# Two transformer blocks on one core: who squares the differential outputs, where gates and root stand among late weight groups, and when the other stream is normed

## The chip, the cores and the metric

The kernel runs on one core of one Trainium2 chip. The metric is the device time of one launch in microseconds (us), as the median of three runs. The program is written by hand: each engine (TensorE or PE, VectorE or DVE, ScalarE or ACT, GpSimd or POOL, and the queue SP that starts weight transfers) has its own list of instructions and they meet at semaphores.

## What is computed

Two blocks follow each other on 256 tokens of width 1024, all in fp32. The change touches the first block alone. Its reference, cut to what matters:

```python
for l in range(DEPTH):                       # 2 layers; ctx first, then x; the second ctx is cut short
    co_ret  = from_heads(rms_norm(c_ret)) * silu(c_rg)
    co_diff = from_heads(rms_norm(c_diff) * (1.0 - lam_init)) * silu(c_dg)
    co_mlp  = u * (w_s @ layer_norm(v) + b_s) * silu(gate)
    # the same three branches on x: o_ret, o_diff, o_mlp
    y   = sigmoid(g_ret)*(o_ret @ w_bo[0]) + sigmoid(g_mlp)*(o_mlp @ w_bo[1]) + sigmoid(g_diff)*(o_diff @ w_bo[2])
    out = y @ w_o
    x   = x + gate * rms_norm(out, g_post[l])
```

`rms_norm` divides each head's 128 numbers by the root of their mean square.

## The kernel before

**Passes.** `PASSES` (L338) runs the first block as four passes n = 0 to 3: ctx and x of layer 0, ctx of layer 1 (only keys, values and states, "not full"), x of layer 1. So three passes are full, and only these hold the code of the change.

**Weights.** Each weight is taken in slabs of 256 x 512 (512 KB). SP loads a slab into `raw` (four slots), ACT copies it to `whi` in fp32r (`split`, L475), POOL subtracts to get the rest `wlo` (L463), and PE multiplies with the high and low parts of weights and activations: three matmuls of 512 columns for each of 2 x 2 blocks, 12 in a slab (`product`, L1455; `slab`, L1461). Four slabs make a chunk of 512 outputs, whose two PSUM banks (one for each 128 tokens) ACT copies out. ACT may split the next slab into a slot once PE has finished the slab there (`weights_used`).

**Late slabs.** In a full pass 44 slabs (11 chunks) are "late": they are dealt one by one among the attention steps, so that PE has work while ACT and DVE do softmax. The order is written out by hand, the same in all engines. `late_slab(n)` on ACT (L501) waits for PE to finish slab n and splits the slab that follows in that slot; when n is the last of a chunk (n = 3 mod 4) it first copies the chunk's two banks out, which PE needs free (`late_evacuated`, waited for in `slab`) before the next chunk's slab 0. All late chunks use the banks G[2:4]. Chunks 0 to 4 are MV, RG, DG, MU, MG; chunks 5 to 10 are the merge gates 0 to 5. Slabs 0 to 9 go beside retention, 10 to 33 beside the eight differential steps (L762), and 34 to 43 after them.

**After the differential steps (before the change).** ACT (L794 to L823) goes through slab 34, SiLU of MG, slab 35 with the copy of chunk 8, SiLU of RG, slab 36, SiLU of DG, slab 37, the square root for the head norms (`rms`, L800), slab 38, Sigmoid of gate 0, slab 39 with the copy of chunk 9 and so on. DVE (L1278 to L1301) waits for the last differential output, squares and sums it (`squares(2, 8)`, L1238 and L1239), forms the MLP branch (L1286, L1290), waits for the root, scales both normed branches by its reciprocal (L1297) and multiplies with their gates (L1301). Three increments of `branches_ready` let PE (L1772) turn the branches: 16 transposes, slab 42, 8 transposes, slab 43. ACT and DVE split the turned tiles to `ohi`, `olo` (L548, L1039).

**Merge** (L553, L1054, L1562). Six units u of two slabs: branch times `w_branch_out`, DVE multiplies with gate and adds; then `w_out`. Between the branches' split and unit 0, ACT (L819) and DVE (L1057) norm the other stream, cx or x, in passes 0 and 1, for the next pass: two squares, root, reciprocal, two products into `normed`. PE turns `normed` at the start of the next pass (L1624). `junk` and `normed` lie over the branches' buffer `o`.

Of the kernel before, what the change touches and what calls it, by code (L numbers as in the profile page):

```python
# [139 lines left out]
def build(nc, g, out):  # L140
# [14 lines left out]
    with ExitStack() as ctx:  # L155
# [311 lines left out]
        def _(act):  # L467
# [85 lines left out]
            def merge(more, in_first, final=False):  # L553
                for u in range(6):
                    act.wait_ge(weights_used, w(weights_used))
                    split(2 * (u % 2))
                    act.wait_ge(branch_out, w(branch_out, TT))
                    split(2 * (u % 2) + 1)
                    if u == 4:
                        split_high(two_kt(hhi)[0:2])  # L560
                for s in range(SLOTS):
# [63 lines left out]
            for n, (is_x, l, full) in enumerate(PASSES):  # L625
# [136 lines left out]
                for i in range(m + 2):  # L762
                    if i >= 2:
                        h, t = divmod(i - 2, TT)
                        act.wait_ge(diff_out, w(diff_out))
                        act.activation(o[:, 2, t, h * P:(h + 1) * P], G[i % 2][:, 0:P], ACT.Copy).then_inc(diff_read, 1)
                    if i < m:
# [25 lines left out]

                act.wait_ge(late_evacuated, w(late_evacuated, len(LATE) * TT))  # L794
                for i, c in enumerate((MG, RG, DG)):
                    late_slab(late + i, late_dst, G[2:4])
                    silu(c)
                late_slab(late + 3, late_dst, G[2:4])
                act.wait_ge(ss_ready, w(ss_ready))
                act.activation(rms[:], ss[:], ACT.Sqrt, bias=eps[:], scale=1.0 / P).then_inc(rms_ready, 1)  # L800
                act.wait_ge(late_evacuated, w(late_evacuated, 4 * TT))
                late_slab(late + 4, late_dst, G[2:4])
                sigmoid(0)
                late_slab(late + 5, late_dst, G[2:4], func=ACT.Sigmoid)
                sigmoid(2)
                late_slab(late + 6, late_dst, G[2:4])
                sigmoid(1)
                late_slab(late + 7, late_dst, G[2:4])
                sigmoid(3)
# [5 lines left out]
                w(late_evacuated, 2 * TT)  # L815
                if n == 0:
                    act.wait_ge(x_in, w(x_in, 16))
                if n < 2:
                    norm(cx if is_x else x)  # L819
                act.wait_ge(branches_ready, w(branches_ready, 3))  # L820
                merge(True, True, n == 3)
# [124 lines left out]
        def _(dve):  # L946
# [107 lines left out]
            def merge(gate, part, then_norm=None, direct=()):  # L1054
                split_low([ap for b in range(3) for ap in two_kt(ohi[:, b], 4)],
                          [ap for b in range(3) for ap in two_kt(olo[:, b], 4)])
                if then_norm is not None:  # L1057
                    norm(then_norm)
# [16 lines left out]
                split_low(two_kt(hhi)[2:4], two_kt(hlo)[2:4], 2)  # L1075

# [53 lines left out]
            for n, (is_x, l, full) in enumerate(PASSES):  # L1130
# [123 lines left out]
                for i in range(m + 1):  # L1254
# [14 lines left out]
                    if i == 3:  # L1269
                        link(squares(0, 0))  # L1270
# [7 lines left out]
                dve.wait_ge(diff_read, w(diff_read, m))  # L1278
                squares(2, 8).then_inc(ss_ready, 1)
                dve.wait_ge(mlp_vn, w(mlp_vn))  # L1280
# [8 lines left out]
                dve.wait_ge(gates_ready, w(gates_ready))  # L1289
                dve.tensor_tensor(o[:, 1], o[:, 1], z[:, :, MG:MG + W], ALU.mult).then_inc(branches_ready, 1)  # L1290

                dve.wait_ge(rms_ready, w(rms_ready))
                link(dve.reciprocal(rstd[:], rms[:]))
                link(dve.tensor_scalar(rstd[:, 8:16], rstd[:, 8:16], 1.0 - (0.8 - 0.6 * math.exp(-0.3 * l)), None, ALU.mult))
                for b, at in ((0, 0), (2, 8)):
                    ob = o[:, b].rearrange("p t (h n) -> p (t h) n", h=H1)
                    ins = dve.tensor_tensor(ob, ob, rstd[:, at:at + 8].unsqueeze(2).to_broadcast([P, 8, P]), ALU.mult)  # L1297
                link(ins)
                for b, gate in ((0, RG), (2, DG)):
                    dve.wait_ge(gates_ready, w(gates_ready))  # L1300
                    dve.tensor_tensor(o[:, b], o[:, b], z[:, :, gate:gate + W], ALU.mult).then_inc(branches_ready, 1)  # L1301
                w(late_evacuated, (1 + 4) * TT)
                if n == 0:
                    dve.wait_ge(x_in, w(x_in, 16))
                merge(lambda c, t: z[:, t, GATE_HOMES[c]:GATE_HOMES[c] + W], lambda t, h: z[:, t, Y_HOMES[h]:Y_HOMES[h] + W],
                      (x, cx, None, None)[n], (2, 5))
# [145 lines left out]
        def _(pe):  # L1452
# [156 lines left out]
            for n, (is_x, l, full) in enumerate(PASSES):  # L1609
# [119 lines left out]
                for i in range(m + 1):  # L1729
# [13 lines left out]
                    if i >= 1:  # L1743
# [10 lines left out]
                        if j >= 2:  # L1754
                            pe.wait_ge(diff_read, w(diff_read))
# [15 lines left out]
                pe.wait_ge(diff_read, w(diff_read, 2))  # L1771
# [196 lines left out]
```

## Time and profile before

| | |
|---|---|
| Median of three runs | 2044.94 us (2044.02 to 2046.29) |
| Profiled execution: its own time | 2043.11 us |
| Profiled execution: span of the instructions | 2041.3 us |
| Mean granted TensorE clock | 0.981 |
| PE busy | 1934.3 us (95%) |
| POOL / ACT / DVE busy | 1375.0 (67%) / 1101.8 (54%) / 614.3 us (30%) |

All times within the kernel are us from the start of the span of this one execution. A matmul's row shows about 0.39 us though the next one starts 0.23 us later, since they are pipelined; so what one slab takes is read from start to start. The three full passes come to the changed code at about 257, 569 and 936 us.

### The profile page before, as it was taken

Reading aid. Unit: us, or ns where it says so; the run is one execution under the profiler, and the core shown is the slowest. Engines: PE = TensorE matmul, PEld = TensorE weight load, DVE = VectorE, ACT = ScalarE, POOL = GpSimd, SP = SyncE. Lnnn points to the kernel's source line nnn. Section 1 sums busy time; section 2 is a strip of 40 time slices with the busy share of each in tenths; the row PEclk is TensorE's granted clock in tenths of the full one; section 3 lists DMA queues with packets and bytes.
Section 4 is the critical chain, followed back from the end, with each engine's and each line's share of the span. In section 5 each row is a group of like instructions: output and inputs, shape, how many; then the busy total and the mean of one; then the engine's idle time right before and its main releaser. Section 6 shows DMA issues by size and latency. Waiting matters only on the chain.

```text
span 2041.3 us, 26146 instructions
## 1 busy us (share of the span) xinstructions
PE 1934.3 (95%) x9524; PEld 1560.7 (76%) x9524; DVE 614.3 (30%) x1123; ACT 1101.8 (54%) x1584; POOL 1375.0 (67%) x573
## 2 busy tenths in 40 slices
PE   6999999999999799999989899999999999999997
PEld 3667877787778678777878677788888777788885
DVE  3212453512342552334325321421113331232111
ACT  3544675334574654466454874554445585555443
POOL 3656778756668667667868444678888744478884
PEclk8999999999999899999989999999999999999999
DMA  9855546744545545444546333356655633345563
GB/s 360 285 195 145 165 147 190 241 124 134 144 145 178 178 125 165 144 135 147 174 124 200 115 93 99 128 175 186 185 176 151 184 94 94 102 156 177 184 185 112
DMA packets 170816, 328.66 MB, mean 161 GB/s; under 512 B 12384, under 2 KB 13536, under 8 KB 170464
## 3 DMA queue, kind: packets, MB, share of 16 engines
q1 hardware_dynamic: 167968, 320.49, 51.3%
q10 hardware_dynamic: 2752, 6.84, 0.9%
q8 instruction: 67, 1.10, 0.2%
q14 instruction: 29, 0.24, 0.0%
HBM read 326.24 MB, written 1.05 MB: 160 GB/s over the span
## 4 chain that ended last, share of the span: by engine, by line
PE 68%; issue 12%; POOL 12%; ACT 4%; DVE 2%; DMA 2%; POOLq 0%; SPq 0%; DVEq 0%; ACTq 0%
PE G L1457 17%; PE G L1459 16%; PE G L1458 16%; POOL wlo L463 12%; PE A L1457 3%; PE A L1458 3%; PE A L1459 3%; PE A L1511 1%; ACT whi L477 1%; PE A L1548 1%; DMA raw<-in_w_in 1%; DMA modz<-in_w_mod 1%; PE A L1737 1%; ACT t L543 1%; PE G L1758 1%
## 5 line engine op out<-in xcount | busy, mean ns | idle before, releaser
L463 POOL TENSOR_TENSOR wlo<-raw,whi 128x1024 fp32r<-128x1024 f32 x568 | 1371.2, 2421 | 643.7 <-ACT whi L477 640.3
L477 ACT ACTIVATE whi<-raw 128x1024 fp32r<-128x1024 f32 x568 | 599.6, 1058 | 685.0 <-PE G L1459 567.8
L1457 PE MATMUL G<-whi,hhi 128*128 128x512 f32 (+1 forms) x1648 | 665.2, 404 | 28.9 <-DVE hlo L971 11.6
L1459 PE MATMUL G<-whi,hlo 128*128 128x512 f32 (+1 forms) x1648 | 645.9, 392 | 0.0
L1458 PE MATMUL G<-wlo,hhi 128*128 128x512 f32 (+1 forms) x1648 | 645.2, 391 | 0.0
L1457 PEld LDWEIGHTS G<-whi,hhi 128*128 128x128 f32 x1648 | 313.8, 190 | 114.9 <-issue 42.9
L1459 PEld LDWEIGHTS G<-whi,hlo 128*128 128x128 f32 x1648 | 313.6, 190 | 67.0
L1458 PEld LDWEIGHTS G<-wlo,hhi 128*128 128x128 f32 x1648 | 314.5, 191 | 59.2
L1457 PE MATMUL G<-whi,ohi 128*128 128x512 f32 x240 | 94.1, 392 | 1.0 <-issue 1.0
L1459 PE MATMUL G<-whi,olo 128*128 128x512 f32 x240 | 93.4, 389 | 0.0
L1458 PE MATMUL G<-wlo,ohi 128*128 128x512 f32 x240 | 93.4, 389 | 0.0
L1258 DVE TENSOR_REDUCE nmx<-A 128x1 f32<-128x512 f32 (+1 forms) x48 | 26.7, 597 | 137.6 <-PE A L1737 137.6
L1457 PEld LDWEIGHTS G<-whi,ohi 128*128 128x128 f32 x240 | 45.1, 188 | 10.9 <-issue 1.8
L1457 PE MATMUL A<-whi,uhi 128*128 128x512 f32 x128 | 50.0, 390 | 3.2 <-DVE ulo L1424 3.2
L1459 PEld LDWEIGHTS G<-whi,olo 128*128 128x128 f32 x240 | 45.0, 188 | 9.4
L1458 PEld LDWEIGHTS G<-wlo,ohi 128*128 128x128 f32 x240 | 45.1, 188 | 9.0
L1457 PE MATMUL A<-whi,hhi 128*128 128x512 f32 x128 | 50.5, 394 | 0.0
L1459 PE MATMUL A<-whi,hlo 128*128 128x512 f32 x128 | 49.9, 390 | 0.0
L1458 PE MATMUL A<-wlo,hhi 128*128 128x512 f32 x128 | 49.8, 389 | 0.0
L1458 PE MATMUL A<-wlo,uhi 128*128 128x512 f32 x128 | 49.8, 389 | 0.0
L1459 PE MATMUL G<-whi,ulo 128*128 128x512 f32 x128 | 49.8, 389 | 0.0
L1459 PE MATMUL A<-whi,ulo 128*128 128x512 f32 x128 | 49.8, 389 | 0.0
(369 smaller groups left out, 2255.4 us busy)
## 6 DMA issues: line engine op xcount, KB each, us to landing
raw<-in_w_in SPq DMA_DIRECT2D x332, 512.0 KB, 3.7
raw<-in_w_up SPq DMA_DIRECT2D x64, 512.0 KB, 3.7
raw<-in_w_down SPq DMA_DIRECT2D x64, 512.0 KB, 3.5
raw<-in_w_out SPq DMA_DIRECT2D x40, 512.0 KB, 3.9
raw<-in_w_branch_out SPq DMA_DIRECT2D x36, 512.0 KB, 3.9
modw<-in_w_mod SPq DMA_DIRECT2D x32, 512.0 KB, 4.9
raw<-in_w_branch SPq DMA_DIRECT2D x24, 512.0 KB, 3.5
modz<-in_w_mod SPq DMA_DIRECT2D x16, 512.0 KB, 11.0
```

Source lines behind the costliest of these rows:

```text
L463: pool.tensor_tensor(wlo[:, s], raw[:, s], whi[:, s].bitcast(F32), ALU.subtract).then_inc(lo_ready, 1)
L477: act.activation(whi[:, slot], raw[:, slot], ACT.Copy).then_inc(hi_ready, 1)
L543: act.activation(dst, A[n % 4][:, 0:dst.shape[-1]], ACT.Copy, scale=scale).then_inc(turned_copied, 1)
L1258: ins = dve.reduce_max(nmx[:, i % 2, b:b + 1], A[2 * (i % 2) + b][:, 0:nk], AX.X, negate=True)
L1457: pe.matmul(bank, hi, whi[:, slot, kk, 0:n], start=first, stop=False)
L1458: pe.matmul(bank, hi, wlo[:, slot, kk, 0:n], start=False, stop=False)
L1459: return pe.matmul(bank, lo, whi[:, slot, kk, 0:n], start=False, stop=last)
L1511: ins = pe.transpose(A[n % 4][:, b * S + t * P:b * S + (t + 1) * P], srcs[2 * (n - bank) + b](t), ident)
L1548: ins = pe.matmul(bank[at:at + 32, 0:MODN], cond[:, q * SLAB_K + kk], ring[:, i % size, kk, h * MODN:(h + 1) * MODN], start=q == 0, stop=q ...
L1737: ins = pe.matmul(bank[:, c * S:(c + 1) * S], dqT[half_p, h, t * P:(t + 1) * P], kT[half_p, h], start=True, stop=True)
L1758: ins = pe.matmul(G[j % 2][:, 0:P], aT[:, j % 2, b * P:(b + 1) * P], val[:, h * P:(h + 1) * P], start=b == 0, stop=b == nb - 1)
```

## The change

In the differential steps ACT squares each output tile from PSUM itself, with the row sum as accumulator output, right behind the copy; DVE's `squares(2, 8)` goes. After the steps ACT takes the root first, then goes through the late slabs with no table function ahead of a chunk's copies; chunk 9 (gate 4) is copied raw and gets its Sigmoid later with gates 0 and 2; the Sigmoids of gates 1 and 3 and the norm of the other stream move into the merge's units 0, 1 and 2. DVE scales the normed branches before the MLP branch, takes MG's gate last, and norms the other stream at the end of its merge. PE's waits on `diff_read` count two per output.

```diff
@@ ACT, merge
-            def merge(more, in_first, final=False):
+            def merge(more, in_first, final=False, beside=None):
                 for u in range(6):
...
+                    if beside is not None:
+                        beside(u)
@@ ACT, differential steps
                         act.activation(o[:, 2, t, h * P:(h + 1) * P], G[i % 2][:, 0:P], ACT.Copy).then_inc(diff_read, 1)
+                        act.activation(rtmp[:, 2 + t, h * P:(h + 1) * P], G[i % 2][:, 0:P], ACT.Square,
+                                       accum_out=ss[:, 8 + t * H1 + h:9 + t * H1 + h]).then_inc(diff_read, 1)
@@ ACT, after them
+                act.wait_ge(ss_ready, w(ss_ready))
+                act.wait_ge(diff_read, w(diff_read, 2 * m))
+                act.activation(rms[:], ss[:], ACT.Sqrt, bias=eps[:], scale=1.0 / P).then_inc(rms_ready, 1)
                 act.wait_ge(late_evacuated, w(late_evacuated, len(LATE) * TT))
-                for i, c in enumerate((MG, RG, DG)):
+                late_slab(late, late_dst, G[2:4])
+                for i, c in enumerate((RG, DG, MG)):
+                    late_slab(late + 1 + i, late_dst, G[2:4])
+                    silu(c)
+                for i in (4, 5):
                     late_slab(late + i, late_dst, G[2:4])
-                    silu(c)
-                late_slab(late + 3, late_dst, G[2:4])
-                act.wait_ge(ss_ready, w(ss_ready))
-                act.activation(rms[:], ss[:], ACT.Sqrt, bias=eps[:], scale=1.0 / P).then_inc(rms_ready, 1)
-                act.wait_ge(late_evacuated, w(late_evacuated, 4 * TT))
-                late_slab(late + 4, late_dst, G[2:4])
+                act.wait_ge(late_evacuated, w(late_evacuated, 5 * TT))
                 sigmoid(0)
-                late_slab(late + 5, late_dst, G[2:4], func=ACT.Sigmoid)
+                late_slab(late + 6, late_dst, G[2:4])
                 sigmoid(2)
-                late_slab(late + 6, late_dst, G[2:4])
-                sigmoid(1)
+                sigmoid(4)
                 late_slab(late + 7, late_dst, G[2:4])
-                sigmoid(3)
...
-                if n == 0:
-                    act.wait_ge(x_in, w(x_in, 16))
-                if n < 2:
-                    norm(cx if is_x else x)
+                def beside_merge(u):
+                    if u < 2:
+                        sigmoid(1 + 2 * u)
+                    if u == 2 and n == 0:
+                        act.wait_ge(x_in, w(x_in, 16))
+                    if u == 2 and n < 2:
+                        norm(cx if is_x else x)
...
-                merge(True, True, n == 3)
+                merge(True, True, n == 3, beside_merge)
@@ DVE, merge
-                if then_norm is not None:
-                    norm(then_norm)
                 for u in range(6):
...
                 split_low(two_kt(hhi)[2:4], two_kt(hlo)[2:4], 2)
+                if then_norm is not None:
+                    norm(then_norm)
@@ DVE, after the differential steps
-                        link(squares(0, 0))
+                        squares(0, 0).then_inc(ss_ready, 1)
...
-                dve.wait_ge(diff_read, w(diff_read, m))
-                squares(2, 8).then_inc(ss_ready, 1)
+                dve.wait_ge(diff_read, w(diff_read, 2 * m))
+                # here now: wait for rms_ready, reciprocal, factor, the two products o * rstd (L1292 to L1298)
...
-                dve.tensor_tensor(o[:, 1], o[:, 1], z[:, :, MG:MG + W], ALU.mult).then_inc(branches_ready, 1)
...
-                for b, gate in ((0, RG), (2, DG)):
+                for b, gate in ((0, RG), (2, DG), (1, MG)):
...
-                      (x, cx, None, None)[n], (2, 5))
+                      (x, cx, None, None)[n], (5,))
@@ PE
-                            pe.wait_ge(diff_read, w(diff_read))
+                            pe.wait_ge(diff_read, w(diff_read, 2))
...
-                pe.wait_ge(diff_read, w(diff_read, 2))
+                pe.wait_ge(diff_read, w(diff_read, 4))
```

The line that begins with # in the diff stands for four lines moved up unchanged.

## Rows read from the trace of the kernel before

**Rows 1.** Page: chain of work that ended last, share of the span.

```profile
PE 68%; issue 12%; POOL 12%; ACT 4%; DVE 2%; DMA 2%; POOLq 0%; SPq 0%; DVEq 0%; ACTq 0%
```

**Rows 2.** One stretch: busy us (x instructions), PE clock, DMA share, GB/s.

```profile
257.00:300.00 43.00, 39.81 (x195) 32.70 (x194) 23.52 (x27) 33.85 (x43) 29.95 (x12) 1.00 0.48 149
```

**Rows 3.** Waits of PE, 255 to 345: total us, times, longest.

```profile
PE G L1457 <- ACT z L509: 2.9, 2, 1.4
PE A L1511 <- DVE o L1301: 0.3, 1, 0.3
```

**Rows 4.** Timeline of PE, pass 0: start, us, instruction [idle before].

```profile
237.56 0.39 PE L1457 MATMUL G<-whi,hhi 128*128 128x512 f32 x1
...
263.88 0.39 PE L1459 MATMUL G<-whi,hlo 128*128 128x512 f32 x1
265.70 0.47 PE L1457 MATMUL G<-whi,hhi 128*128 128x512 f32 x1 [1.43 <-ACT z L509]
...
268.55 0.39 PE L1457 MATMUL G<-whi,hhi 128*128 128x512 f32 x1
...
271.26 0.39 PE L1457 MATMUL G<-whi,hhi 128*128 128x512 f32 x1
...
284.35 1.94 PE L1511 MATMUL A<-const,o 128*128 128x128 f32 x16 [0.33 <-DVE o L1301]
...
295.20 0.39 PE L1457 MATMUL G<-whi,ohi 128*128 128x512 f32 x1
...
351.32 1.09 PE L1525 MATMUL A<-const,normed 128*128 128x128 f32 x8 [0.69 <-ACT oproj L591]
```

**Rows 5.** Timeline of ACT, pass 0.

```profile
237.76 0.60 ACT L509 ACTIVATE z<-G 128x512 f32<-128x512 f32 x1 [0.63 <-PE G L1459]
...
261.64 1.06 ACT L477 ACTIVATE whi<-raw 128x1024 fp32r<-128x1024 f32 x1 [3.79 <-issue]
262.72 1.28 ACT L788 ACT_TABLE_LOAD   x1
264.01 1.06 ACT L788 ACTIVATE z<-z 128x1024 f32<-128x1024 f32 x1
264.98 1.07 ACT L509 ACTIVATE z<-G 128x512 f32<-128x512 f32 x2
...
273.84 0.31 ACT L800 ACTIVATE rms<-ss,eps 128x16 f32<-128x16 f32 x1
...
297.96 1.99 ACT L477 ACTIVATE whi<-raw 128x1024 fp32r<-128x1024 f32 x2
```

**Rows 6.** Timeline of DVE, pass 0.

```profile
257.88 3.35 DVE L1238 TENSOR_TENSOR rtmp<-o 128x1024 f32<-128x1024 f32 x1 [9.08 <-ACT o L766]
...
275.06 4.53 DVE L1297 TENSOR_TENSOR o<-o,rstd 128x1024 f32<-128x1024 f32 x2
279.62 4.58 DVE L1301 TENSOR_TENSOR o<-o,z 128x1024 f32<-128x1024 f32 x2
...
334.51 1.29 DVE L1039 TENSOR_TENSOR hlo<-A,hhi 128x512 fp32r<-128x512 f32 x2 [6.83 <-ACT hhi L548]
```

**Rows 7.** Groups of ACT's copy and square accumulator: ns min/median/max.

```profile
L766 ACT ACTIVATE o<-G x24: 256/260/268, 195.8 to 935.8; 128x128 f32<-128x128 f32 x24
...
L523 ACT ACTIVATION_READ_ACCUMULATOR junk<-x x14: 184/187/250, 295.1 to 2033.2; 128x1 f32 x14
```

**Rows 8.** Waits of ACT's exponentials, pass 0, then pass 1.

```profile
ACT e L770 <- DVE nmx L1258: 2.8, 5, 0.7
...
ACT e L770 <- DVE nmx L1258: 8.7, 5, 2.1
```

**Rows 9.** Timeline of ACT at the start: an Exp, then a Square.

```profile
10.53 0.20 ACT L621 ACTIVATE lam<-lam 128x4 f32<-128x4 f32 x1 [0.57 <-DVE lam L1089]
12.97 1.06 ACT L523 ACTIVATE junk<-cx 128x1024 f32<-128x1024 f32 x1 [2.23 <-DMA cx<-in_ctx]
```

**Rows 10.** Timeline of POOL in pass 0's merge.

```profile
299.08 24.35 POOL L463 TENSOR_TENSOR wlo<-raw,whi 128x1024 fp32r<-128x1024 f32 x10 [2.37 <-ACT whi L477]
```

More of the change, by code:

```diff
@@ L814, in _ @@
                 late_slab(late + 9, late_dst, G[2:4], func=ACT.Sigmoid)
-                w(late_evacuated, 2 * TT)
-                if n == 0:
-                    act.wait_ge(x_in, w(x_in, 16))
-                if n < 2:
-                    norm(cx if is_x else x)
+                w(late_evacuated, TT)
+                def beside_merge(u):
[5 more added lines that the diff above has]
+                        norm(cx if is_x else x)
                 act.wait_ge(branches_ready, w(branches_ready, 3))
-                merge(True, True, n == 3)
+                merge(True, True, n == 3, beside_merge)
                 if n < 3:
@@ L1277, in _ @@
                         ins.then_inc(mlp_vn, 1)
-                dve.wait_ge(diff_read, w(diff_read, m))
-                squares(2, 8).then_inc(ss_ready, 1)
-                dve.wait_ge(mlp_vn, w(mlp_vn))
+                dve.wait_ge(diff_read, w(diff_read, 2 * m))
+                dve.wait_ge(rms_ready, w(rms_ready))
+                link(dve.reciprocal(rstd[:], rms[:]))
+                link(dve.tensor_scalar(rstd[:, 8:16], rstd[:, 8:16], 1.0 - (0.8 - 0.6 * math.exp(-0.3 * l)), None, ALU.mult))
+                for b, at in ((0, 0), (2, 8)):
+                    ob = o[:, b].rearrange("p t (h n) -> p (t h) n", h=H1)
+                    dve.tensor_tensor(ob, ob, rstd[:, at:at + 8].unsqueeze(2).to_broadcast([P, 8, P]), ALU.mult).then_inc(dve_step, 1)
+                dve.wait_ge(dve_step, w(dve_step, 2))
                 dve.wait_ge(late_evacuated, w(late_evacuated, 3 * TT))
@@ L1288, in _ @@
                     link(ins)
-                dve.wait_ge(gates_ready, w(gates_ready))
-                dve.tensor_tensor(o[:, 1], o[:, 1], z[:, :, MG:MG + W], ALU.mult).then_inc(branches_ready, 1)
[L1292 to L1298, printed above, removed]
-                for b, gate in ((0, RG), (2, DG)):
+                for b, gate in ((0, RG), (2, DG), (1, MG)):
                     dve.wait_ge(gates_ready, w(gates_ready))
                     dve.tensor_tensor(o[:, b], o[:, b], z[:, :, gate:gate + W], ALU.mult).then_inc(branches_ready, 1)
-                w(late_evacuated, (1 + 4) * TT)
+                w(late_evacuated, (1 + 5) * TT)
                 if n == 0:
```

## Prediction

> **What bounds the kernel.** I read the chain of work first: two thirds of the span are PE, the rest small pieces [rows 1]. So an edit on ACT or DVE is worth only the PE pauses it ends. Next the stretch that the change touches: in 43 us from 257, PE is busy for 39.81, ACT for 33.85, DVE for 23.52, POOL for 29.95, at a granted clock of 1.00 [rows 2]; the same 43 us in the other two full passes show 39.82 both times. The stage is PE's, and 3.2 us of it are pauses. The list of PE's waits names them: twice a matmul waited for the copy of a late chunk (L509), once the transposes waited for DVE's last gate product (L1301) [rows 3]. The other two full passes have these lines with the same numbers; there is no other PE wait up to 345.
>
> **What a pause costs.** The rows overlap, so I go from start to start [rows 4]. From 268.55 to 271.26 a slab takes 2.71, 0.226 a matmul. Across the first pause the starts are 263.88 and 265.70, 1.82 apart: 1.82 - 0.23 = 1.59 lost. The slab behind it takes 268.55 - 265.70 = 2.85, another 0.13: matmuls restart slowly. Together 1.72, and twice 3.44. The transposes show 0.33 idle; with the overlap of 0.39 - 0.23 = 0.16, 0.49 are lost. They start slowly anyway. A pass pays 3.44 + 0.49 = 3.93, three passes 11.8 us. That is all that the edits can win on PE here.
>
> **Why the first pause goes.** PE pauses because ACT holds the copy of chunk 8 [rows 5]: split of slab 34 at 261.64, table load 1.28, SiLU of MG 1.06, and only at 264.98 the two copies, although the first bank was done half a slab earlier. A copy that nothing precedes is early enough: at 237.76 ACT took the second bank's copy as soon as PE had finished it (idle 0.63 until then), and PE, already in the next chunk since 237.56, shows no pause [rows 4, 5]. In the new order slab 34 is followed by slab 35 with its copies. ACT idles 3.79 before 261.64, and the root now stands there: the load 1.28 and 0.31. So PE goes on at 264.11, and the second copy starts at 264.3.
>
> **The second pause** comes from the first Sigmoid in front of chunk 9's copies, a table load and 1.06 again. It goes if ACT has caught up by then. I roll ACT forward from 264.3 with 0.95 from one large activation to the next (264.01 to 264.98, [rows 5]) and slabs of 2.72. Slab 36 now runs from 264.11, 37 from 266.83, 38 from 269.55, 39 from 272.27, 40 from 274.99, 41 from 277.71 to 280.43. ACT: copy 264.3, split 264.8, load 265.8, SiLU RG 267.1, split 268.1 (due 267.0), SiLU DG 269.0, split 270.0 (due 269.8), SiLU MG 270.9, split 272.5 on time, copies 273.8 and 275.2 on time. Both pauses are gone.
>
> **The third pause.** DVE made branches ready from the root at 273.84, by two products (4.53) and two gate products (4.58) [rows 5, 6]. Now the root ends near 259.8; DVE no longer spends 3.35 and the reduction after it on squares, and has its products done by 265.3, the MLP branch by 267.6. Then it follows ACT's gates: RG 268.1, DG 270.0, MG 271.9, each with one product of at most 3.4 (the slow one of each pair), so the last is ready by about 275.5. PE asks at 280.43. Margin 5 us.
>
> **What is late next.** After slab 39: split 275.7, load 276.7, Sigmoid 0 at 278.0, split 279.0 (due 277.9), Sigmoids 2 and 4, split 281.8 (due 280.6). Splits 1.2 us late do no harm: a slot has three slabs of 2.72 = 8.2 us between its release and its use, of which split and POOL take 1.06 + 2.43 (24.35 over 10, [rows 10]), 4.7 us of slack. ACT then starts the four high parts at 282.8, 2.3 behind the transposes' start, against 1.6 now. PE's second transposes need DVE's first low part at 284.9, after slab 42; it ends at 282.8 + 0.6 + 0.7 = 284.1. That margin, 0.8 us, is the thinnest of the plan. I cost it at nothing; if ACT is 1.5 us later than I think, it costs 0.7 a pass.
>
> **The squares on ACT.** Each adds a 128x128 activation of 0.26 and an accumulator read of 0.19, 0.45 us [rows 7], 24 times: 10.8 us of ACT. That is the upper bound if all of it were exposed; zero is the lower. Behind the copy ACT waits for DVE's maxima anyhow: in pass 0 five waits, 2.8 in total, up to 0.7; in pass 1 five, 8.7 in total, up to 2.1 [rows 8]; pass 3 has 2.1 for the longest too. These hold 0.45 each except at one or two steps of pass 0, where 0.3 to 0.45 shift splits with slack. Who waits behind it on ACT is the exponential, then DVE's mix, then transposes two slabs later. PE's doubled count on `diff_read` refers to outputs two steps back, some 10 us earlier. I take zero. Table loads: no Square of the trace has one in front. The first follows an Exp at 10.53 with no load between [rows 9], which is the case of these steps.
>
> **The merge.** Now ACT's norm (two squares, load, root, 4 us) precedes unit 0, and the split at 297.96 comes 2.5 late, for PE ended unit 0's first slab at 295.20 + 0.23 [rows 4, 5]. POOL then runs ten subtractions without a break [rows 10], and still PE waits for nothing. In unit 2 the norm delays a split by just as much, once; units 0 and 1 have 5.44 us of PE for 2.1 of splits and 0.95 of a Sigmoid. Gate 1 is needed in unit 3, gate 3 in unit 4. So the move neither wins nor loses. DVE's norm now runs behind its last split product at 334.51 + 1.29 [rows 6]; `normed` is then ready by 338 to 340, and PE turns it at 351.32 [rows 4], 11 us later. In pass 3 there is no norm. Weights' transfers follow POOL, and no queue gets more of them.
>
> **A rule of the skill that speaks against it.** A table load shows 1.28 us and the SiLU starts at 264.01, 0.01 behind its end; nothing drains in between [rows 5]. The Trainium skill, "ScalarE: Activation LUTs", section "What ACT_TABLE_LOAD costs", gives 1.28 us for the load and about 1.38 us of drain, 2.66 us a switch. By it, SiLU's and Sigmoid's loads would put the high parts 2.8 us later, and 0.7 or more a pass would be lost at PE's second transposes; the row speaks against it, and the sum goes by the row.
>
> **Sum.** -11.8 us + 0 for the squares + 0 for the merge. On the profiled execution, 2043.11 (span 2041.3 and 1.8 around it), that gives 2031.3. The median of the three runs is 1.8 above it, and their spread is 2.3; I predict on the median's scale: 2044.94 - 11.8 = 2033.1.
>
> **Rivals.**
> A (forecast, 0.72): all three pauses go: 2033.1, own range 2031 to 2036.
> B (0.16): part of it comes back. Either a copy of chunk 9 is still late, since ACT carries a backlog through three SiLUs (1.72 a pass, 5.2), or the high parts come late behind three Sigmoids (0.7 to 1.5 a pass, 2 to 4.5). For it: ACT is busy for 33.85 of 43 us, and the 0.8 us margin. Against it: splits released by PE find ACT again by slab 38. 2035 to 2038.5.
> C (0.04): a table switch costs ACT more than its row, by up to another 1.28 at each of the two loads. The high parts come 2.6 later, 1.8 past the margin: 1.8 x 3 = 5.4 of 11.8 are lost, 2038.5. Against it: the 0.01 above. This is what the skill's drain would do.
> D (0.05): nothing is won, since PE's pauses were POOL's time to catch up. POOL needs 2.43 of each 2.72 [rows 10]; if DVE's five large products, now closer together, slowed it by 1 us each, it would fall behind by more than the 4.7 of slack, and PE would stop for it. Against it: POOL is busy for 29.95 of 43 us here [rows 2] and waited 2.37 for ACT before its run of ten. 2044 to 2045.
> E (0.03), the other side: Square is not in the table set of Exp, so each of the 24 brings two loads, 2.56 more, 3.0 with its own 0.45. The exponential then starts 3.0 - 0.7 = 2.3 later in pass 0 and 3.0 - 2.1 = 0.9 later in passes 1 and 3; if PE waits each time, 8 x 2.3 + 16 x 0.9 = 33, less 11.8: 2066. It decides once more than a third of that reaches PE. Against it: rows 9.
>
> **Numbers.** The mean granted clock is 0.981 over the whole and 1.00 here [rows 2], so it is lower in places elsewhere, and how much of PE's work falls into these may change when everything after 264 comes 4 to 12 us earlier; with the runs' spread I put 2 us on either side for it. Low end: A with that, 2030.8. High end: B and C, 2038.6; outside are D, E and the tails. A measurement of this kernel tells about 0.2%, 4 us: faster (below 2040.9) holds A, B and C, 0.92; within, D, 0.05; slower, E, 0.03.
>
> **What would show it.** Right: in the stretch from 257 PE's waits on L509 and on DVE's gate product are gone, its transposes start near 280.4, the merge's first matmul comes 3.9 us earlier in pass 0, 7.9 in pass 1, 11.8 in pass 3, and all later stages keep their lengths. ACT's load of the Sqrt table lies before slab 34's split, with no load in front of a Square. Wrong: any PE wait on `ohi`/`olo` products or on POOL behind slab 41 (B, D), a load at each Square (E), a gap behind the loads (C), or a PE wait for `normed` at the pass's end.

## Result and profile after

The changed kernel takes 2032.99 us (median of 6 runs, 2027.88 to 2036.08), the kernel before, beside it on the same chip, 2044.48 (6 runs, 2039.66 to 2046.29): a ratio of 0.9948, 95% interval 0.9937 to 0.9960. The forecast was 2033.1, from a gain of 11.8 us; the medians stand 11.5 apart. The profiled execution took 2032.57, its span 2030.8.

First PE's waits in the stretch of the change. From 255 to 345 the list of the kernel after is empty; the three waits of [rows 3] are gone. The same stretch as [rows 2] (columns: stretch, length, busy us of PE, PE's weight loads, DVE, ACT, POOL, then PE clock, DMA share, GB/s):

```profile
257.00:300.00 43.00, 43.00 (x214) 36.28 (x213) 17.51 (x23) 32.02 (x45) 35.06 (x15) 1.00 0.53 162
```

PE is busy for all 43.00, where it was for 39.81; the counterpart in pass 1, from 569, reads 43.00 too. DVE has 6 us less to do; POOL has 15 instructions in the stretch, where it had 12, and 5 us more.

The page's chain of work that ended last, against [rows 1]:

```profile
PE 43%; issue 26%; POOL 26%; ACT 3%; POOLq 1%; DVE 1%; DMA 0%; DVEq 0%; ACTq 0%
```

PE's share fell from 68 to 43% and POOL's rose from 12 to 26%, in a kernel whose PE is busy for 95% as before and whose PE waits only became fewer. The chain follows whichever releaser came last, and its shares do not follow the time: of the kernels below, one that is slower than the kernel before (order alone) has the same 43 and 26%, one 9 us faster than it (the first with a held split) has 90% for PE. Nothing is read from these shares here; PE's waits decide.

ACT in pass 0, against [rows 5] (start, us, instruction, idle before):

```profile
260.61 0.26 ACT L768 ACTIVATE o<-G 128x128 f32<-128x128 f32 x1
260.77 0.27 ACT L769 ACTIVATE rtmp<-G 128x128 f32<-128x128 f32 x1
...
261.20 1.28 ACT L800 ACT_TABLE_LOAD   x1
262.50 0.31 ACT L800 ACTIVATE rms<-ss,eps 128x16 f32<-128x16 f32 x1
...
265.97 0.60 ACT L509 ACTIVATE z<-G 128x512 f32<-128x512 f32 x1 [0.25 <-PE G L1464]
267.33 0.60 ACT L509 ACTIVATE z<-G 128x512 f32<-128x512 f32 x1 [0.76 <-PE G L1464]
...
270.19 1.06 ACT L792 ACTIVATE z<-z 128x1024 f32<-128x1024 f32 x1
...
276.85 0.60 ACT L509 ACTIVATE z<-G 128x512 f32<-128x512 f32 x1 [0.30 <-PE G L1464]
278.21 0.60 ACT L509 ACTIVATE z<-G 128x512 f32<-128x512 f32 x1 [0.76 <-PE G L1464]
...
285.83 2.04 ACT L548 ACTIVATE ohi<-A 128x512 fp32r<-128x512 f32 x4
```

The root lies before all that slab 34 and those behind it put on ACT. Both pairs of copies (265.97 and 267.33; 276.85 and 278.21) now follow PE: each starts when PE has finished its bank, with ACT idle ahead of it. No table load stands in front of the Square at 260.77.

DVE, against [rows 6] (same columns):

```profile
263.40 2.36 DVE L1294 TENSOR_TENSOR o<-o,rstd 128x1024 f32<-128x1024 f32 x2
265.80 2.29 DVE L1301 SCALAR_TENSOR_TENSOR o<-A,small,z 128x128 f32<-128x128 f32 x8
271.36 1.23 DVE L1306 TENSOR_TENSOR o<-o,z 128x1024 f32<-128x1024 f32 x1 [3.28 <-ACT z L792]
273.18 6.09 DVE L1306 TENSOR_TENSOR o<-o,z 128x1024 f32<-128x1024 f32 x2 [0.59 <-ACT z L792]
286.51 2.48 DVE L1049 TENSOR_TENSOR olo<-A,ohi 128x512 fp32r<-128x512 f32 x4 [7.23 <-ACT ohi L548]
```

POOL, in the same stretch:

```profile
272.28 16.40 POOL L463 TENSOR_TENSOR wlo<-raw,whi 128x1024 fp32r<-128x1024 f32 x6 [0.92 <-ACT whi L477]
```

Six subtractions took 16.40, 2.0 more than six times the 2.40 of one that no product of DVE meets. What DVE and POOL do to each other is taken up at the end.

And PE's two groups of transposes, against [rows 4]:

```profile
283.46 1.91 PE L1516 MATMUL A<-const,o 128*128 128x128 f32 x16
...
287.95 1.03 PE L1516 MATMUL A<-const,o 128*128 128x128 f32 x8
```

**Stages of both profiled executions**, from PE's starts (us). Three marks a pass: "mix", the first matmul of the mixing (`z,wsT`); "turn", the first transpose of the branches; "end", the first transpose of the next pass (of `x` behind pass 3). "Pass 2 and its ends" runs from the first transpose of pass 2 to that of pass 3. In the kernel before the marks are at 256.87, 284.35 and 351.32 in pass 0.

```
                      before   after   difference
start to mix, pass 0  256.87  259.89   +3.02
mix to turn, pass 0    27.48   23.57   -3.91
turn to end, pass 0    66.97   66.94   -0.03
end to mix, pass 1    217.64  220.41   +2.77
mix to turn, pass 1    27.48   23.57   -3.91
turn to end, pass 1    66.97   66.95   -0.02
pass 2 and its ends    68.63   65.90   -2.73
to mix, pass 3        203.52  203.52    0.00
mix to turn, pass 3    27.48   23.57   -3.91
turn to end, pass 3    74.26   74.35   +0.09
the rest             1004.00 1002.14   -1.86
span                 2041.3  2030.8   -10.5
```

The whole gain is the three times -3.91; the other rows sum up to +1.2. Those that move by 2 or 3 are not the change's: a second profiled execution of the same changed kernel (below) has 256.64, 217.24 and 66.64 in the first, fourth and seventh. What moved them is PE's granted clock. Before the mixing of pass 0 it reads 0.50, the lower level of 1.2 GHz, from 37.15 to 47.39 in the kernel before and from 33.69 to 50.75 in the changed kernel: 6.8 us more at half speed, for the +3.02. The +2.77 and the -2.73 go the same way: 3.4 us at 0.50 before against 10.2 after, and 13.7 against 6.8.

### The profile page after: what moved, and what is told of

Its sections match the earlier page's. It is cut to its first block, busy times and chain, and to the rows that moved or that the text cites. A ratio compares the mean times of both kernels' runs of the same rounds, so it can differ in the third digit from the quotient of the medians.

```text
span 2030.8 us, 26191 instructions
## 1 busy us (share of the span) xinstructions
PE 1933.4 (95%) x9524; PEld 1562.3 (77%) x9524; DVE 601.4 (30%) x1117; ACT 1110.9 (55%) x1635; POOL 1372.2 (68%) x573
## 4 chain that ended last, share of the span: by engine, by line
PE 43%; issue 26%; POOL 26%; ACT 3%; POOLq 1%; DVE 1%; DMA 0%; DVEq 0%; ACTq 0%
POOL wlo L463 26%; PE G L1462 9%; PE G L1464 9%; PE G L1463 9%; PE A L1462 3%; PE A L1464 3%; PE A L1463 3%; ACT whi L477 1%; ACT t L543 1%; PE A L1516 1%; PE A L1851 0%; PE A L1850 0%; PE A L1849 0%; ACT L875 0%; PE G L1911 0%
## 5 line engine op out<-in xcount | busy, mean ns | idle before, releaser
L509 ACT ACTIVATE z<-G 128x512 f32<-128x512 f32 x66 | 38.8, 597 | 27.1 <-PE G L1464 27.1
```

The source lines that it names most:

```text
L509: act.activation(dst[c][t], banks[t][:], func, scale=1.0 if scale is None else scale[t])\
```

## Experiments

All ratios are to the kernel before, run beside the kernel on the same chip, with 95% intervals. "Mix to turn" and "turn to end" are the stages above. The edits are shown shortened: arguments that all calls share are left out, and lines that begin with # tell the rest in words.

### Which part wins: the root's chain or the order of the late slabs

**Root and squares alone.** The changed kernel with ACT's old order of late slabs, and chunk 9 copied with the Sigmoid as before:

```diff
  # kept: root first; Square on ACT; DVE's products first, MG's gate last; norm in the merge
- late_slab(late)
- for i, c in enumerate((RG, DG, MG)): late_slab(late + 1 + i); silu(c)
- late_slab(late + 4); late_slab(late + 5)
- sigmoid(0); late_slab(late + 6); sigmoid(2); sigmoid(4); late_slab(late + 7)
- # sigmoid(1), sigmoid(3) beside units 0 and 1
+ for i, c in enumerate((RG, DG, MG)): late_slab(late + i); silu(c)
+ late_slab(late + 3); late_slab(late + 4)
+ sigmoid(0); late_slab(late + 5, func=ACT.Sigmoid); sigmoid(2)
+ late_slab(late + 6); sigmoid(1); late_slab(late + 7); sigmoid(3)
```

> Kernel after, with the old order of ACT's late part (a SiLU behind slab 34, a Sigmoid ahead of chunk 9's copies, Sigmoids 1 and 3 ahead of the branches' split); squares on ACT, the root first and DVE's new order stay: the complement of e1. My theory (the edits gain only together: copies free PE, the early root lets it go on): both pauses at L509 stay at 1.4, the third goes, the stretch from mixing to the transposes is 27.0 against 27.5 before and 23.6 after, the whole 1 to 2 us under before: 2042. Rival (the root's load between slabs 37 and 38 was half of the second pause): that pause shrinks by 0.5 or more, the stretch is 26.5 or less, 2040.

2040.72 us, ratio 0.9991 (0.9982 to 1.0000). Mix to turn took 26.99 in all three passes, 0.49 less than before, the price that the prediction put on the third pause. PE's waits from 255 to 345 (releaser, total us, times, longest): DVE's line is gone, the copies' stays.

```profile
PE G L1461 <- ACT z L509: 2.9, 2, 1.4
```

**Order alone.** The kernel before with ACT's new order, root still behind slab 37:

```diff
+ late_slab(late)
  for i, c in enumerate((MG, RG, DG)):
-     late_slab(late + i)
+     late_slab(late + 1 + i)
      silu(c)
- late_slab(late + 3)
  rms = Sqrt(...)
  late_slab(late + 4)
- sigmoid(0); late_slab(late + 5, func=Sigmoid); sigmoid(2)
- late_slab(late + 6); sigmoid(1); late_slab(late + 7); sigmoid(3)
+ late_slab(late + 5, func=Copy); sigmoid(0)
+ late_slab(late + 6); sigmoid(2); sigmoid(4); late_slab(late + 7)
+ # sigmoid(1), sigmoid(3) beside units 0 and 1
```

> Kernel before, with the new order of copies, SiLUs and Sigmoids among slabs 34 to 43 (Sigmoids 1 and 3 in the merge); squares stay on DVE, the root stays behind slab 37, the norm stays ahead of the merge. My theory (the chain from the root to the branches is late next): the two pauses at L509 go (3.44 us a pass), but the root still ends near 272.5, DVE's products and gate products end near 283, and PE, which now asks near 280.4, waits some 3 us for L1301; a full pass's stretch from the last differential copy to the transposes of normed shrinks from 93.7 by 0.7 to 1.2 us, the whole by about 3: 2041. Rival (the order of the copies is the whole gain, early root and squares are beside the point): no wait on DVE, 3.44 a pass, 10.3 in all: 2034.

2053.09 us, ratio 1.0047 (1.0030 to 1.0063): slower than before, against both expectations. The two waits on the copies are gone, and one of 4.7 on DVE's gate product stands in their place (waits of PE, 255 to 345):

```profile
PE A L1512 <- DVE o L1302: 4.7, 1, 4.7
```

The root ends at 275.53, after a load of its own behind two SiLUs, and DVE has 11.2 us of products left. All four overlap POOL's subtractions; one took 1.23, the other three 3.3 to 3.4 each (DVE's timeline, then POOL's):

```profile
275.56 0.25 DVE L1294 RECIPROCAL rstd<-rms 128x16 f32<-128x16 f32 x1 [4.11 <-ACT rms L802]
276.14 4.58 DVE L1298 TENSOR_TENSOR o<-o,rstd 128x1024 f32<-128x1024 f32 x2
280.75 6.60 DVE L1302 TENSOR_TENSOR o<-o,z 128x1024 f32<-128x1024 f32 x2
```
```profile
276.56 12.99 POOL L463 TENSOR_TENSOR wlo<-raw,whi 128x1024 fp32r<-128x1024 f32 x4 [0.48 <-ACT whi L477]
```

Mix to turn came to 28.75, 1.27 more than before, and turn to end grew too, by 1.7, 2.8 and 2.1 in passes 0, 1 and 3. A window of pass 0 behind the wait shows with what (columns as above):

```profile
287.50:290.91 3.41, 3.41 (x17) 3.41 (x17) 1.38 (x2) 1.78 (x3) 2.05 (x1) 0.50 0.50 154
```

Behind the 4.7 us in which PE stood still, its granted clock is 0.50 for 3.4 us, the lower level of 1.2 GHz; in passes 1 and 3 it is 0.50 for 6.8 us, from 601.53 and from 970.17, still within the wait. Behind the pauses of 1.6 us in the kernel before it stayed at 1.00 [rows 2].

So mix to turn is 27.48 with neither part, 26.99 with the root's chain, 28.75 with the order, 23.57 with both. The gain of 3.91 is no sum of the two: ending the copies' pauses moves PE's request for the branches forward to where only an early root can serve it. "The root's chain" is here all of the change but ACT's order: the runs below that put the squares and the norm back show that these two are not what counts in it; DVE's new order was not tried by itself.

**The first pause alone.** In the kernel before, SiLU of MG moved behind slab 35:

```diff
- for i, c in enumerate((MG, RG, DG)): late_slab(late + i); silu(c)
+ late_slab(late)
+ late_slab(late + 1); silu(MG); silu(RG)
+ late_slab(late + 2); silu(DG)
```

> Kernel before, only with the SiLU of MG moved from ahead of slab 35's copies to behind them. My theory (each pause is worth its 1.59 and a slow slab behind it of 0.13): the first pause goes, the second and third stay as they are, 1.72 a pass, 5.2 in all: 2039.5, stretch 92.0. Rival (a pause removed returns at the next wait, as the third one's chain is late by as much): the wait on L1301 grows by up to 1.7 and the time stays at 2044.

2050.64 us (2045.26 to 2055.18), ratio 1.0041 (1.0019 to 1.0062): slower, against both expectations. The first pause did go, but ACT carried two SiLUs, the root's load and the Sigmoid's to chunk 9. Its timeline in pass 0:

```profile
268.93 2.01 ACT L788 ACTIVATE z<-z 128x1024 f32<-128x1024 f32 x2
...
273.80 1.28 ACT L804 ACT_TABLE_LOAD   x1
...
276.37 1.28 ACT L792 ACT_TABLE_LOAD   x1
...
278.63 1.07 ACT L509 ACTIVATE z<-G 128x512 f32<-128x512 f32 x2
```

The pause at chunk 9 grew from 1.4 to 2.4 in all three passes. In pass 3 alone DVE's product came late too (waits of PE, 920 to 1045):

```profile
PE A L1515 <- DVE o L1305: 3.0, 1, 3.0
PE G L1461 <- ACT z L509: 2.4, 1, 2.4
```

The granted clock fell as in the run above. In pass 0 it did so behind the copies' pause:

```profile
280.41:283.82 3.41, 3.41 (x10) 2.64 (x9) 3.38 (x2) 1.18 (x2) 2.76 (x1) 0.50 0.43 153
```

Pass 1 has the same, from 597.85. In pass 3 the clock stayed at 1.00 behind this pause; so PE came to the transposes before the last gate product was ready (969.88), waited 3.0, and ran at 0.50 from 969.91 to 973.32. Mix to turn grew by 0.44 and 0.42 in passes 0 and 1 and by 1.94 in pass 3, turn to end by 1.76 in pass 3. That is 4.5 us; the span is 7.6 longer. The other 3 lie in stages that vary between executions of one kernel.

### Which parts were not needed

**Norm back ahead of the merge**, on ACT and DVE:

```diff
- if u == 2 and n < 2: norm(cx if is_x else x)   # in beside_merge(u)
+ if n < 2: norm(cx if is_x else x)              # ahead of merge, as before
  # DVE's norm too: from the end of its merge to ahead of unit 0
  merge(True, True, n == 3, beside_merge)  # with sigmoid(1), sigmoid(3) alone
```

> Kernel after, with the norm of the other stream back ahead of the merge on ACT and DVE. My theory: the move cost and won nothing, since a split 2.5 us late is covered by POOL's slack in either place: pass 0's stretch stays at 89.8, the time at 2033, within 1 us, although the Sigmoids of units 0 and 1 now need one more table load of 1.28 a pass. Rival (it freed the merge's start): the stretch grows by 1 us or more in passes 0 and 1, PE waits for a product or for POOL in units 0 to 2, 2035 or more.

2031.99 us, ratio 0.9943 (0.9927 to 0.9960): the changed kernel's time. Mix to turn is 23.57 and turn to end 66.93 in pass 0, as there, though the Sigmoid of gate 1 needs a load more behind the norm's root (ACT, pass 0):

```profile
293.70 0.30 ACT L525 ACTIVATE rms<-ss,eps 128x2 f32<-128x2 f32 x1
...
295.91 1.28 ACT L796 ACT_TABLE_LOAD   x1
```

PE waits for nothing there. The norm's place is worth nothing either way.

**Squares back on DVE**, all else changed:

```diff
- act.activation(rtmp, G[i % 2][:, 0:P], ACT.Square, accum_out=ss[...])
+ squares(2, 8).then_inc(ss_ready, 1)      # DVE, behind the last output
- act.wait_ge(ss_ready, w(ss_ready)); act.wait_ge(diff_read, w(diff_read, 2 * m))
+ act.wait_ge(ss_ready, w(ss_ready, 2))    # ahead of the root
```

> Kernel after, with the squares of the differential outputs back on DVE (two instructions behind the last output) and ACT's root waiting for them. My theory: DVE's squares end 4.6 us behind the last copy, the root ends near 264.1 in the times of before, so slab 34's split is 2.5 us late and the first copy of chunk 8 is 2.2 us late: the first pause comes back, 1.6 to 1.9 a pass, about 5 in all: 2038. Rival (DVE has time, the squares could stay there): the stretch stays at 89.8 and the time at 2033.

2032.39 us, ratio 0.9944 (0.9927 to 0.9960): my expectation was wrong, the rival's right. ACT's timeline shows why:

```profile
260.39 1.28 ACT L797 ACT_TABLE_LOAD   x1
265.04 0.31 ACT L797 ACTIVATE rms<-ss,eps 128x16 f32<-128x16 f32 x1 [3.36 <-DVE ss L1246]
...
266.20 1.24 ACT L509 ACTIVATE z<-G 128x512 f32<-128x512 f32 x2
```

The load had run while the root waited for DVE's sum, so the root ended 1.3 us earlier than I had reckoned. The two copies stand together behind it and are late by 0.4 in pass 0 alone (mix to turn 23.97), on time in passes 1 and 3 (23.60, 23.59). So ACT's Square is not what wins; the root's place ahead of the late slabs is, and DVE's squares would have allowed it.

### How thin the margins are

**More table loads at the differential steps**, to price rival E and the drain of rival C:

```diff
+ act.activation(mx8[:, 0, 0:1], eps[:], ACT.Sqrt)
  act.activation(o[:, 2, t, h * P:(h + 1) * P], G[i % 2][:, 0:P], ACT.Copy)
  act.activation(rtmp[...], G[i % 2][:, 0:P], ACT.Square, accum_out=ss[...])
```

> Kernel after, with a root of one number ahead of each of the 24 output copies, so that each step loads the Sqrt table and then the Exp table again: what rival E of the prediction would have done (2.57 us and a small activation more in each step). My theory (PE sees ACT only where a chunk's copies are late): in passes 1 and 3 the two pauses of 0.67 at the copies of steps 2 and 6 grow by about 1.1 each, in pass 0 two pauses of some 2 us appear, 8 to 9 us in all over the kernel after: 2041.5. Rival (the exponentials are on PE's path, as in the prediction's E): 33 us more, 2066; all of it exposed: 67 more, 2100. If the switch costs more than the load's row, a gap stands behind each load.

2047.49 us, ratio 1.0013 (1.0002 to 1.0024). One of the ten executions took 6906.68 us; why is not known, and it is left out of the ratio. The median of the other nine is 2046.81: 14 us more than the changed kernel, 13 by the ratios, where I had expected 8 to 9. The trace has 100 table loads, 30 more than the changed kernel's 70, and not the 48 that the edit was meant to add: 18 of Sqrt and 15 of Exp more, 3 fewer ahead of the roots. Where a step has no exponential between two of the added roots, or a Sqrt already precedes one, none is needed. ACT, pass 0:

```profile
198.37 1.28 ACT L768 ACT_TABLE_LOAD   x1
199.66 0.20 ACT L768 ACTIVATE mx<-eps 128x1 f32<-128x1 f32 x1
...
200.31 1.28 ACT L775 ACT_TABLE_LOAD   x1
201.61 0.47 ACT L775 ACTIVATE e<-A,nmx 128x256 f32<-128x256 f32 x1
```

Each of these loads ends 0.01 to 0.02 before the next instruction starts; a drain would have stood there. The loads reach PE only through the copies of a chunk: from start to start PE paused for 2.15, 1.77 and 2.15 us at three of them in pass 0, and for 1.68, 1.07 and 1.68 in passes 1 and 3. I had counted two of these three. Behind the first of pass 0 the clock fell as well (window), behind the third, of the same 2.15, it stayed at 1.00:

```profile
203.24:206.65 3.41, 3.39 (x8) 2.73 (x9) 0.00 (x0) 1.31 (x2) 2.02 (x1) 0.50 0.19 74
```

**Sigmoids 1 and 3 ahead of the transposes**, not in the merge; there are five there then, and three in the changed kernel:

```diff
  sigmoid(2); sigmoid(4)
+ sigmoid(1); sigmoid(3)
- # sigmoid(1), sigmoid(3) beside units 0 and 1
```

> Kernel after, with the Sigmoids of gates 1 and 3 ahead of slab 41's split instead of in the merge. My theory: the high parts of the turned branches come 1.9 us later, against a margin of 0.75 us (first low part ends 287.2, PE's second transposes begin 287.95): PE waits 1.1 to 1.4 a pass, 3.3 to 4.2 in all: 2037. Rival (setting gates aside in the merge was not needed): 2033.

2035.12 us, ratio 0.9962 (0.9948 to 0.9976). Turn to end grew by 1.44, 1.34 and 1.32, where the prediction had put the thinnest margin (waits of PE, 255 to 345):

```profile
PE A L1516 <- DVE olo L1049: 1.0, 1, 1.0
```

ACT runs four Sigmoids in one row of 3.89 us here, two more than the changed kernel, 1.9 us; less the 0.8 of margin that is 1.1, and PE waited 1.0.

### A better version

In the attention of passes 1 and 3 PE still waited twice for a chunk's copies (changed kernel, 480 to 610):

```profile
PE G L1462 <- ACT z L509: 1.0, 2, 0.5
```

**Copies first at two steps:**

```diff
+ first = is_x and i in (2, 6)
+ if first: late_slab(late); late += 1     # ahead of the exponentials
  ...
- for _ in range(2): late_slab(...)
+ for _ in range(1 if first else 2): late_slab(...)
```

> Kernel after, and in steps 2 and 6 of the passes on x the slab that ends a chunk (its two copies and its split) stands ahead of the two exponentials on ACT. My theory (the same mechanism as the change: PE's pause is a copy held behind other work on ACT): the pauses of 0.67 at L509 in passes 1 and 3 go, four of them with 0.13 each for the slow slab behind: 3.2 us less than the kernel after: 2029.8. Rival: the exponentials, 2 us later, hold up the mix and the transposes of the next step, and the time stays or grows.

2029.34 us, ratio 0.9926 (0.9911 to 0.9942). By the ratios this is not told apart from the changed kernel's 0.9942 (0.9929 to 0.9955); the gain is read from the trace. Both waits are gone; in pass 3, from the pass's `normed` to mix takes 201.97 instead of 203.52, 1.55 less. Both copies lie ahead of the exponential in pass 1 (ACT):

```profile
499.63 0.60 ACT L509 ACTIVATE z<-G 128x512 f32<-128x512 f32 x1 [2.06 <-PE G L1468]
500.99 0.60 ACT L509 ACTIVATE z<-G 128x512 f32<-128x512 f32 x1 [0.76 <-PE G L1468]
502.44 0.68 ACT L778 ACTIVATE e<-A,nmx 128x512 f32<-128x512 f32 x1
```

**And the first transposes of a pass before ACT's last copy out** of the merge, for which the split of one slab is held back on ACT:

```diff
- pe.wait_ge(out_evacuated, w(out_evacuated, 2 * TT))          # ahead of turn_tokens
+ if q == 2: pe.wait_ge(out_evacuated, w(out_evacuated, 2 * TT))
+ if held and q == 0: split(SLOTS - 1)     # in turned_high, not in the merge
```

> As the run before it, and at the start of passes 1 and 2 PE turns the first half of normed ahead of its wait for the last out copies, and ACT splits the last slab behind the first high parts of the next pass instead of ahead of them. My theory: the pause of 0.85 ahead of the transposes goes and the pause of 2.2 ahead of the next pass's first matmul shrinks by about 1, 2 passes: 3 to 4 us less again: 2026.5. Rival: the second pause is set by DVE's low parts and grows by what the first one loses; only ACT's earlier high parts count, 1 to 2 us: 2028.5.

2033.76 us, ratio 0.9956 (0.9943 to 0.9970): slower than the run above, against both expectations. The step won 0.85 in each of passes 0 and 1 (turn to end 66.09 and 66.10) and lost more behind it. From 340 to 360 PE waited 4.0 us for DVE's low part (2.1 in the run above), and 4.8 for the one near 659 (2.2 there). DVE's timeline and POOL's in both places:

```profile
348.69 2.77 DVE L987 TENSOR_TENSOR hlo<-hfull,hhi 128x512 fp32r<-128x512 f32 x1
...
658.78 2.43 DVE L987 TENSOR_TENSOR hlo<-hfull,hhi 128x512 fp32r<-128x512 f32 x1
```
```profile
348.58 2.34 POOL L463 TENSOR_TENSOR wlo<-raw,whi 128x1024 fp32r<-128x1024 f32 x1 [1.76 <-ACT whi L477]
...
658.32 2.34 POOL L463 TENSOR_TENSOR wlo<-raw,whi 128x1024 fp32r<-128x1024 f32 x1 [2.64 <-ACT whi L477]
```

The same product in the run above (DVE's timeline):

```profile
659.97 0.69 DVE L985 TENSOR_TENSOR hlo<-hfull,hhi 128x512 fp32r<-128x512 f32 x1
```

With the held split it falls into the held slab's subtraction and is done only when that is. "Pass 2 and its ends" grew from 68.46 to 72.28, with a granted clock of 0.89 from 655 to 732 (0.91 in the run above). So the held split goes to the fourth high part instead of the first:

```diff
- if held and q == 0: split(SLOTS - 1)
+ if held and q == 3: split(SLOTS - 1)
```

> As e8, but the held split stands behind the fourth pair of high parts instead of the first, so that POOL's subtraction no longer runs beside DVE's first low part, which took 2.43 instead of 0.69 in e8. My theory (that meeting was e8's loss): the wait for L987 at the start of passes 1 and 2 falls from 4.0 and 4.8 to about 2.1, with no pause ahead of the transposes; 2 us less than e7: 2027.3. Rival (turning normed early and ACT's earlier high parts win nothing as such): 2029.3 or more.

2026.11 us (5 runs, 2023.70 to 2029.67), ratio 0.9924 (0.9911 to 0.9937): the lowest median here, though by its ratio it is not told apart from the copies alone (0.9926), and what the held split adds, 0.8 us by the stages below, is not shown by the times. PE's wait between 340 and 360 is 1.9 again, and turn to end stays at 66.09 and 66.11; the product near 659 still meets POOL (a wait of 3.1, 0.9 more than without the held split). Two times 1.57 from the copies (end to mix 215.67 in pass 1, to mix 201.94 in pass 3, each against the run below) and two times 0.85 less that 0.9 make 3.9; it is 4.0 faster than the changed kernel in the same call. So close a match is in part luck: "pass 2 and its ends" is 2.6 longer than in the run below, most of it at a lower granted clock, and other stages are shorter by as much.

**The changed kernel again**, in one call with the run before it and with "root and squares alone":

> The kernel after itself, on the chip of the two before it, for comparison: 11 to 12 us under the kernel before, 2031 to 2033.

2030.15 us, ratio 0.9942 (0.9929 to 0.9955); the median lies 0.9 below the range that I had given. It shows how far a stage moves with no edit at all. The window from 351 to 435, first of the changed kernel's first execution, then of this one:

```profile
351.00:435.00 84.00, 81.95 (x407) 63.80 (x406) 30.65 (x73) 32.44 (x41) 55.10 (x23) 0.94 0.61 195
```
```profile
351.00:435.00 84.00, 82.63 (x432) 64.73 (x432) 28.65 (x71) 34.61 (x45) 57.87 (x24) 0.98 0.63 201
```

The same program and the same PE waits, but 0.94 against 0.98 of granted clock: "end to mix, pass 1" is 220.41 there and 217.24 here. The first execution has two stretches at 0.50 in this window, 10.2 us together, the second one of 3.4 us:

```profile
354.54:357.95 3.41, 3.41 (x9) 2.63 (x10) 3.34 (x8) 2.88 (x6) 0.00 (x0) 0.50 0.53 154
415.98:422.80 6.82, 6.82 (x22) 5.66 (x22) 0.62 (x4) 0.00 (x0) 0.00 (x0) 0.50 0.25 77
```
```profile
411.89:415.30 3.41, 3.41 (x10) 2.76 (x10) 0.63 (x4) 0.00 (x0) 0.00 (x0) 0.50 0.38 138
```

Why the clock falls more often in one execution than in another is open.

## Why the prediction was right

The kernel entered the stage 3.02 us later than the forecast had it, all of that ahead of the change; in the second execution it entered 0.23 earlier, and the transposes start at 280.21. With 3.02 taken off, pass 0 of the first against the plan:

```
                                predicted  measured - 3.02
root done                         259.8      259.8   (262.50 + 0.31)
MLP branch formed                 267.6      265.1   (265.80 + 2.29)
SiLU of RG done                   268.1      268.2   (270.19 + 1.06)
last gate product ready           275.5      276.3   (273.18 + 6.09)
PE's first transposes             280.43     280.44  (283.46)
ACT's high parts                  282.8      282.8   (285.83)
DVE's first low part done         284.1      284.2   (286.51 + 0.69)
PE's second transposes            284.9      284.9   (287.95)
```

- **What a pause costs:** 3.93 a pass predicted from start to start, 3.91 measured in each of three passes. The idle times in the waits list (2.9 and 0.3, together 3.2) would have given 9.6 for three passes and missed the slow restart and the overlap of rows.
- **First and second pause:** the copies follow PE as said. But the prediction reads as if the first were won by the moved SiLU alone. The run with that edit alone shows that the backlog goes on to chunk 9. It takes the rest of ACT's new order, with no Sigmoid ahead of chunk 9's copies, to lose it: with that order PE waited for none of these copies even with the root still late. The early root is then what keeps DVE's chain from taking their place.
- **Third pause:** right; priced at 0.49, and the root's chain alone gave 0.49. DVE's margin is 4.2 us (283.46 - 279.27), not 5: the last two gate products took 6.09 beside POOL, where I had one slow product at each gate of at most 3.4 and ACT's gates in between.
- **What is late next:** the 0.8 at PE's second transposes is what was measured, and the run with four Sigmoids in a row used it up and lost 1.0 at just that wait.
- **Squares on ACT at zero:** right. The attention before the mixing, where they stand, is no longer: 203.52 before and after in pass 3, 203.53 with the squares on DVE. What the prediction left unsaid is that they were not needed either.
- **Merge at zero:** right, by the run with the norm put back.
- **The two rules on tables.** In the kernel before [rows 5], after it, and with the added loads, every load is followed by its activation within 0.02, but for five in each trace whose activation waited for another engine: the drain of rival C is not there. The Trainium skill, "ScalarE: Activation LUTs", section "What ACT_TABLE_LOAD costs", has 1.38 us of it; the traces disagree. Rival E's Square had no load in 24 places. Its price was too high: 30 more loads at these steps cost 13 to 14 us, where the prediction had 33 for two at each of 24. Part of the difference is the number of loads, part that they reach PE only at the chunks' copies and not at each exponential.
- **Rival D's slowing where DVE and POOL meet** exists, and on both sides. DVE's last two gate products took 2.76 and 3.41, and the two subtractions beside them that start at 274.81 and 278.15 took 3.38 each instead of 2.40, the 1 us that D had put on each. D was wrong in what follows: POOL lost 2.0 us in the whole run of six, less than the 4.7 of slack, and PE waited for neither engine. The meeting is part of what sank the order alone.
- **Merge, DVE's part:** `normed` was forecast for 338 to 340 and is ready at 336.4 in an execution that is 3.02 late, PE turns it at 350.40; so there was more room than planned.
- **Sum:** -11.7 in the stages, +1.2 elsewhere in the profiled execution, -11.5 by the medians. That the median came within 0.1 us of 2033.1 is luck: the six executions span 8 us, and the second call's median is 2030.15. The mechanism rests on the three times -3.91. The 2 us on either side for where the clock falls were about right: single stages moved by 3, the sum by 1.2. In the stage of the change it was 1.00 before and after.

## What to carry to other kernels

Price a pause of PE from matmul start to matmul start across it, not by the idle time in a waits list, and roll the engine that caused it forward through the next two deadlines before calling it gone: an edit that ends one pause can hand its backlog to the next, and two edits that gain 3.9 together gained 0.5 and lost 1.3 (more behind it) alone. In this kernel, copies that free a PSUM bank belong first on their engine, table functions behind them. When work is moved, look at which of DVE's products with two SBUF operands will then run beside POOL: both engines lose time there.

## What was not expected of the hardware

**DVE beside POOL.** The gate products of the changed kernel (min, median and max in ns, times of the first and last start):

```profile
L1306 DVE TENSOR_TENSOR o<-o,z x9: 1227/2754/3412, 271.4 to 946.7; 128x1024 f32<-128x1024 f32 x9
```

One and the same shape takes 1.23 us with POOL idle for all but its last 0.3 us (271.36 above) and up to 3.41 when it meets a subtraction of POOL's; one of 128x512 takes 0.69, or 2.43 and 2.77. The rows look as if it waited rather than ran slowly: in the kernel with the held split the two products end at 351.46 and 661.21, POOL's instructions at 350.92 and 660.66, so 0.54 and 0.55 earlier, little less than such a product takes alone. POOL pays as well: a subtraction that starts while DVE's product is under way took 3.38 in place of 2.40. The Trainium skill, "SBUF — State Buffer", section "SBUF: two separate sides", calls the port pair that the two share an exclusive lock, whose loser fully blocks, and counts a DVE instruction with two SBUF inputs among those that need it. The traces of these two rows agree.

**The clock behind longer pauses.** Behind a loss of 4.8 us (from start to start) in the run with the order alone, 3.1 and 2.6 in the run with the moved SiLU and 2.15 in the run with added loads, the granted clock was 0.50 for 3.4 us, in two cases 6.8; 3.4 us at half speed cost PE another 1.7. Behind the pauses of 1.6 in the kernel before it read 1.00 [rows 2]. Between these the length does not decide: the 2.6 left it at 1.00 in pass 3, the second 2.15 of the run with added loads did too, and in the kernel before, of two equal waits of 2.05 for DVE's low part, the one that ended at 355.34 left it at 1.00 and the one that ended at 667.42 was followed by 3.4 us at 0.50. What else decides was not tried.

**A table load does not wait.** It runs ahead of the semaphore that its activation waits for: load at 260.39, activation at 265.04, released by DVE. There the root waited 4.65 from the start of its load, so the load of 1.28 cost it nothing.
